# Expert rows beyond the first 128 in units of 32 rows, computed in float32 on four column tiles

## The reference, cut to what matters

```python
def expert_block(args):
    xb, e = args
    return (jax.nn.silu(xb @ w1_l[e]) * (xb @ w3_l[e])) @ w2_l[e]
```

```
135 135 153 129 194 186 171  89 103 161 174  73  77  88 155 115
145  78 135 127 141 177 113 138 161 102  85 101 134 120 112 105
```

## Time and profile before

| | |
|---|---|
| median of three runs | 2259.6 us |
| the profiled execution | 2255.27 us, of it 2253.7 us from the first to the last instruction (the span) |
| mean granted TensorE clock | 0.977 of 2.4 GHz |
| TensorE busy | 2149.3 us, 95% |
| VectorE, ScalarE, GpSimd busy | 1430.6, 971.0 and 581.7 us |
| moved by DMA | 407 MB, 181 GB/s over the span |

### The profile page before, as it was taken

One profiled execution on the slowest core, in us unless ns is written; L12 is line 12 of the kernel. 1 busy time (PEld: TensorE's weight loads), 2 busy tenths in 40 slices (PEclk: granted clock), 3 DMA queues, 4 the chain that ended last, 5 costly groups with the idle time before them and its releaser, 6 DMA issues. The chain is left out here.

```text
span 2253.7 us, 34056 instructions
## 1 busy us (share of the span) xinstructions
PE 2149.3 (95%) x10539; PEld 1773.2 (79%) x10540; DVE 1430.6 (63%) x2866; ACT 971.0 (43%) x1569; POOL 581.7 (26%) x595
## 2 busy tenths in 40 slices
PE   6999999999899999994889999999999999899998
PEld 5878888888788888884778888888888878767775
DVE  5788888888566665564536465665566566846554
ACT  4433344444432222222435465665556465623332
POOL 1121111111244333332121223233332132233332
PEclk9999999999999999996999999999999999999999
DMA  6111110132534333324787677898787778943441
GB/s 231 60 38 66 65 60 37 65 112 92 187 107 136 121 121 117 103 91 147 292 309 256 219 266 289 292 363 289 283 294 260 289 290 305 334 169 125 158 141 49
DMA packets 160333, 407.13 MB, mean 181 GB/s; under 512 B 18835, under 2 KB 22347, under 8 KB 160014
## 3 DMA queue, kind: packets, MB, share of 16 engines
q1 hardware_dynamic: 138518, 337.17, 42.0%
q0 software_dynamic: 14560, 43.11, 5.8%
q10 hardware_dynamic: 7200, 26.22, 2.9%
HBM read 330.12 MB, written 84.82 MB: 184 GB/s over the span
## 5 line engine op out<-in xcount | busy, mean ns | idle before, releaser
L234 PE MATMUL bank<-w_hi,mix_x 128*128 128x512 f32 x816 | 333.3, 408 | 9.9 <-DMA mix_x<-xT_dram 4.0
L236 PE MATMUL bank<-w_hi,mix_x 128*128 128x512 f32 x816 | 323.8, 397 | 0.0
L235 PE MATMUL bank<-w_lo,mix_x 128*128 128x512 f32 x816 | 322.9, 396 | 0.0
L2113 PE MATMUL bank<-w_hi,x_hi 128*128 128x512 f32 x784 | 307.6, 392 | 8.1 <-POOL w_lo L2070 4.6
L2212 DVE TENSOR_TENSOR w_lo<-raw,w_hi 128x2048 fp32r<-128x2048 f32 x130 | 292.6, 2311 | 34.8 <-ACT w_hi L2149 34.7
L2115 PE MATMUL bank<-w_hi,x_lo 128*128 128x512 f32 x784 | 307.1, 392 | 0.0
L2114 PE MATMUL bank<-w_lo,x_hi 128*128 128x512 f32 x784 | 307.1, 392 | 0.0
L2149 ACT ACTIVATE w_hi<-raw 128x2048 fp32r<-128x2048 f32 x130 | 238.8, 1925 | 4.8 <-DMA raw<-in_w 4.8
L2070 POOL TENSOR_TENSOR w_lo<-shared,w_hi 128x2048 fp32r<-128x2048 f32 x31 | 157.2, 5071 | 231.7 <-DMA shared<-hn_dram,entry 131.9
L234 PEld LDWEIGHTS bank<-w_hi,mix_x 128*128 128x128 f32 x816 | 156.7, 192 | 42.0 <-issue 5.1
L236 PEld LDWEIGHTS bank<-w_hi,mix_x 128*128 128x128 f32 x816 | 156.3, 192 | 34.7
(11 more groups left out here) (316 smaller groups left out, 4222.1 us busy)
## 6 DMA issues: line engine op xcount, KB each, us to landing
raw<-in_w SPq DMA_DIRECT2D x128, 1024.0 KB, 8.5
shared<-in_w SPq DMA_DIRECT2D x64, 1024.0 KB, 8.6
y_dram<-y_sb ACTq DMA_DIRECT2D x50, 512.0 KB, 6.9
xT_dram<-mix_x SPq DMA_DIRECT2D x34, 512.0 KB, 3.5
mix_x<-xT_dram SPq DMA_DIRECT2D x34, 512.0 KB, 4.5
shared<-in_w_in SPq DMA_DIRECT2D x24, 512.0 KB, 6.5
small<-in_x_prompt SPq DMA_DIRECT2D x16, 512.0 KB
xr_sb<-in_x_prompt SPq DMA_DIRECT2D x16, 512.0 KB
```

Of the source, the lines that this page charges most:

```text
L234: pe.matmul(bank[:, :], x_hi[:, k, :], wh[:, k, :], start=(k == 0), stop=False)
L235: pe.matmul(bank[:, :], x_hi[:, k, :], wl[:, k, :], start=False, stop=False)
L236: ins = pe.matmul(bank[:, :], x_lo[:, k, :], wh[:, k, :], start=False, stop=(k == KD - 1))
L2113: pe.matmul(bank[:, :], x_hi[:, k, :], wh[:, k, :], start=(k == 0), stop=False)
```

## The change

Every expert has one block of 128 rows now, and its rows beyond 128 go in units ("tails") of 32. `MAXT` is 32 + 4112/32 = 160. An expert has max(1, (rows - 128)/32 rounded up) units: also one with at most 128 rows has one, whose rows nothing reads. Units need no split weights: they multiply plain float32 rows with the raw matrices. All raw matrices stay whole for that: w1 and w3 of two experts (`raw13[0]` and `raw13[1]`), w2 of one (`raw2`). The units of expert e + 1 are computed within expert e's turn, between its H3 matmuls and its second half of Y; those of expert 0 in the turn of expert 31, for which its weights are loaded a second time. There are three slots of split weights in place of four. The first half of Y (12 matmuls, `first_down`) stands inside the unit's code, so it is done again by every unit after an expert's first.

```diff
-MAXBLK = NE + (SEQ + NS) * 2 // P
+TAIL = 32
+TILES = P // TAIL
+MAXT = NE + (SEQ + NS) * 2 // TAIL
-        y_dram = dram("y_dram", ((MAXBLK + 2) * P, D))
+        y_dram = dram("y_dram", (NE * P + (MAXT + 1) * TAIL, D))
...
# DVE, before the expert stage: units of each expert, at least one
-TS(blk[:, 0, :], POS, float(P - 1), None, ALU.add)
+TS(blk[:, 0, :], POS, float(TAIL - 1 - P), None, ALU.add)
-TS(blk[:, 1, :], blk[:, 0, :], 7, None, ALU.arith_shift_right)
+TS(blk[:, 1, :], blk[:, 0, :], 5, None, ALU.arith_shift_right)
 TS(rt[:, 0, :], blk[:, 1, :], 1.0, None, ALU.max)
...
# SP
+def expert(e, two, j):
+    wait_lo(sp_, e, 2, 1)
+    load(behind(e), 1 - j, 2)
+    sp_.wait_ge(h3_mm, e + 1)
+    for m in range(2):
+        if last(e):
+            load_gate(m)
+        else:
+            load(e + 2 if not isinstance(e, int) or e < NE - 2 else 0, j, m)
 sp_.wait_ge(rows_loaded, 16)
-for m in (1, 2):
-    for c in range(2):
-        load(0, m, c)
-reload(1)
-reload(2)
+load(0, 0, 1)
+sp_.wait_ge(lo_ready, 1)
+sp_.wait_ge(w1_lo, 1)
+load(0, 0, 2)
+load(1, 1, 0)
+load(1, 1, 1)
+for e in range(2):
+    expert(e, 0, e)
 total = count_all(sp_)
-with sp_.Fori(total + 1, MAXBLK + 2) as i:
-    sp_.dma_start(y_dram[bass.ds(i * P, P), :], hn_dram[0:P, :]).then_inc(spare_filled, 16)
+with sp_.Fori(total, MAXT + 1) as i:
+    sp_.dma_start(y_dram[bass.ds(i * TAIL + NE * P, TAIL), :], hn_dram[0:TAIL, :]).then_inc(spare_filled, 16)
 with sp_.Fori(0, total) as i:
     sp_.sem_inc(spare_filled, 16)
-with sp_.Fori(3, NE) as e:
-    reload(e)
+with sp_.Fori(1, NE // 2 - 1) as two:
+    for j in range(2):
+        expert(two * 2 + j, two, j)
...
# GpSimd, expert(e): one gather of the block's rows, then one for each unit, then its half of w1
+q = behind(e)
+first, end = span(pool, q)
+if not last(e):
+    gather(e + 1)
+with pool.Fori(first, end) as i:
+    ...
+    gather_tail(i + 1, at + (rest >> (12 * more)))
+if not last(e):
+    split_w1(e + 1, *follow(two, j))
...
# PE, a unit of expert e + 1 in expert e's turn
+def tail(i, e, two, j):
+    for m in range(2):
+        for c in range(2):
+            pe.wait_ge(*tail_in(e, two, j, m, c))
+    pe.wait_ge(t_x_in, i + 1)
+    w13 = raw13[1 - j][:, :].rearrange("p (m k n) -> p m k n", m=2, k=KD)
+    for k in range(KD):
+        for q in range(TILES):
+            ins = pe.matmul(UP_T[q * TAIL:(q + 1) * TAIL, :].rearrange("p (m n) -> p m n", m=2), xT_t[:, k, :],
+                            w13[:, :, k, q * P:(q + 1) * P], start=(k == 0), stop=(k == KD - 1))
+    ins.then_inc(t_up_mm, 1)
+    ...
+    pe.wait_ge(hidT_lo_ready, 2 * e + 2)
+    first_down(0)
+    pe.wait_ge(t_rows, 16 * i + 32)
+    first_down(1)
+    tail_transposes()
+    pe.wait_ge(t_hid, i + 1)
+    pe.transpose(HID_T, hid_t[:, :], ident[:, :]).then_inc(t_hid_tp, 1)
+    first_down(2)
+    first_down(3)
+    for c in range(2):
+        pe.wait_ge(*tail_in(e, two, j, 2, c))
+    pe.wait_ge(t_y_in, i + 1)
+    pe.wait_ge(t_hidT_in, i + 1)
+    ...
+    for k in range(KF):
+        for q in range(TILES):
+            ins = pe.matmul(DOWN_T[q * TAIL:(q + 1) * TAIL, :], hidT_t[:, k * TAIL:(k + 1) * TAIL],
+                            w2[:, k, q * width:(q + 1) * width], start=(k == 0), stop=(k == KF - 1))
+    ins.then_inc(t_down_mm, 1)
...
# ACT, expert(e)
+split(e, two, j, 2)
+act.wait_ge(h1_mm, e + 1)
+act.activation(tanh_h[:, :], H1[:, :], ACT.Tanh, scale=0.5)
+split(e + 1, *follow(two, j), 0)
+for n in range(2):
+    act.wait_ge(hid_tp, 2 * e + n + 1)
+    copy(hidT_hi[:, slice(*K_OF[n]), :], parts_of(AT[n], n))
+if not last(e):
+    x_halves(e + 1)
+with act.Fori(first, end) as i:
+    tail(i, e)                       # tanh, next rows, hidT_t, y_t and its store
+split(e + 1, *follow(two, j), 1)
+for n, done in enumerate((tails_done, y1_mm)):
+    act.wait_ge(done, e + 1)
+    copy(y_sb[:, n * 512:(n + 1) * 512], Y[n][:, :])
```

More of the change, by code:

```diff
@@ L1950, in span, with behind @@
+                (t_entry, t_rows, t_xtp, t_x_in, t_up_mm, t_tanh, t_up, t_hid, t_hid_tp, t_hidT_in, t_down_mm, t_y_in, t_stored) = [sem(n) for n in (
+                    "t_entry t_rows t_xtp t_x_in t_up_mm t_tanh t_up t_hid t_hid_tp t_hidT_in t_down_mm t_y_in t_stored").split()]
+                def behind(e):
+                    return 0 if isinstance(e, int) and e == NE - 1 else e + 1
                 def span(eng, e):
-                    first = eng.value_load(blk[0:1, 0, bass.ds(e, 1)], min_val=0, max_val=MAXBLK - 1)
@@ L2108, in block_of, with expert @@
+                        def expert(e, two, j):
+                            first, end = span(pe, behind(e))
+                            pe.wait_ge(xe_lo_ready, 2 * e + 2)
                             for m, (bank, done) in enumerate(((H1, h1_mm), (H3, h3_mm))):
@@ L2242, in choices_rows, with expert @@
                             dve.wait_ge(place_steps, 4)
-                            STT(yrow[:, :, :], rowbase[:, :, :], float(P), place[:, :, :], ALU.add, ALU.add).then_inc(place_steps, 1)
+                            STT(yrow[:, :, :], rowbase[:, :, :], float(-NE * (CAP - P) - P), place[:, :, :], ALU.add, ALU.add).then_inc(place_steps, 1)
                             dve.wait_ge(place_steps, 5)
-                        def after(e, j, end):
-                            if isinstance(e, int) and e == NE - 1:
+                        def expert(e, two, j):
+                            first, end = span(dve, behind(e))
+                            if last(e):
+                                dve.wait_ge(xe_tp, NE)
@@ L2248, in after @@
                                 choices_rows()
-                            for part in parts_ahead(e, j):
-                                theirs = part[2] == 0 and not (isinstance(e, int) and e + 2 == NE and part[0] == NE)
-                                split(*part, halves=(0,) if theirs else (0, 1))
-                        split(0, 0, 0)
+                            split(e, two, j, 2)
+                            dve.wait_ge(tanh_done, e + 1)
+                            STT(up[:, :], tanh_h[:, :], 1.0, H1[:, :], ALU.add, ALU.mult).then_inc(up_done, 1)
@@ L2254, in _ @@
+                            split(e + 1, *follow(two, j), 0, (0, 1) if last(e) else (0,))
+                            with dve.Fori(first, end) as i:
+                                tail(i)
+                            if not last(e):
+                                x_halves(e + 1)
+                            split(e + 1, *follow(two, j), 1)
+                        split(0, 0, 0, 0)
                         x_halves(0)
-                        split(0, 0, 1)
-                        split(0, 0, 2)
@@ L2257, in _ @@
-                        all_blocks(dve, block_of, after)
+                        split(0, 0, 0, 1)
+                        each_expert(dve, expert)
         with ExitStack() as late:
```

422 lines of the change are left out of this document (238 added, 184 removed).

## The result

| | kernel before | changed kernel | forecast |
|---|---|---|---|
| median of the runs, us | 2260.06 (2258.1 to 2264.37, 4 runs) | 2505.98 (2500.84 to 2513.0, 4 runs) | 2377 |
| ratio to before | 1 | 1.109 [1.105, 1.112] | 1.052 |
| span of the profiled execution, us | 2253.7 | 2511.3 | |
| expert stage, us | 904.0 | 1149.5 | 1021 |
| mean granted clock | 0.977 | 0.936 | |

What follows compares the result with a forecast made beforehand. TensorE was taken to bound the expert stage. Terms 7 + 100 - 7 + 2 + 4 + 11 = +117 us on 2255.3 make 2372; the median lies 4.3 higher, so 2377 us. Own range 2305 to 2430; 8-in-10 range 2295 to 2575.

Steps and rivals of the forecast that it cites:

- The other engines: Expert turns: ScalarE some 16 us, VectorE about the same, loads 20.8 us, all hidden under TensorE's 25.0 us; nothing charged.
- In order of time ScalarE is the closest: ScalarE's w3 high parts behind a unit's down: low part ready after about 7 us, H3 begins after 8.1; nothing charged.
- a wait for ScalarE in every turn, say: Example of outcomes lying between the forecast and rival 1, given a chance of 0.07.
- The start: First unit of the expert stage: TensorE waits for w3 of expert 1, +4 us.
- The fills: 121 fills on the SP queue delay w2 of expert 3, stalling TensorE in expert 2's turn, +100 us.
- Rival 3: The fills hold nothing up: 2275 us, or 2231 us with units at full streaming; chance 0.08.
- TensorE's work: Expert stage: 32 blocks, 40 units of 7.2 us and repeated `first_down`, 879 us in place of 872, +7 us.
- Rivals 1 and 2: Units' column tiles overlap by pairs only (2561 us, chance 0.27), or not at all (2940 us, chance 0.05).
- The issue rate: Units' matmuls: 0.071 us a record, so 64 up records take at least 4.5 us; 3.9 was taken.
- rival 1: Units' column tiles overlap by pairs only: up 7.0 us, unit 12.0 us, total 2561 us; chance 0.27.
- The end: Last turn: late gate load and split delay `first_down` by 9 us and the last `y_sb` by 2, +11 us.
- low end: Forecast's own range: 2305 us with full streaming, 82 us of fill stall and 5 at the end.

Runs made afterwards that it cites:

- run 2: Changed kernel with ScalarE splitting the next w2 right behind `y_sb`, ahead of its store and the register loads; 2471.8 us, ratio 1.094.
- run 5: Changed kernel with GpSimd's waits for gather landings moved to just ahead of the next list load; 2499.4 us, ratio 1.105.
- run 7: Changed kernel with both ScalarE's earlier w2 split and GpSimd's later landing waits; 2383.6 us, ratio 1.055.
- run 4: Changed kernel with 31 larger fills, earlier w2 split, first unit's transposes behind H3, last turn's gate splits behind its unit; 2397.0 us, ratio 1.060.
- run 8: Changed kernel with ScalarE's and GpSimd's orders mended, fills in the mixer's 16 steps, last turn and start reordered; 2278.4 us, ratio 1.008.
- run 12: Changed kernel with ScalarE's and GpSimd's orders, last turn and start mended, and one 512 KB fill behind each turn's loads; 2261.5 us, ratio 1.0002.
- run 1: Changed kernel with 31 fills of 512 KB in place of 121 of 128 KB; 2432.8 us, ratio 1.076.
- run 6: Changed kernel with all fills moved to the token mixer's stage, 322 rows in each of 16 steps; 2413.6 us, ratio 1.068.
- run 3: Changed kernel with column tiles outermost in the up matmuls, k inside; 2790.9 us, ratio 1.235.
- run 9: As run 8, with the mixer's fills in its first 14 steps, 368 rows each; 2283.6 us, ratio 1.010.

## Why the prediction was right and wrong

**The failed step: "The other engines", and in it "In order of time ScalarE is the closest … I charge nothing; if it came 1 us late in each turn it would cost 32."** The turn was taken as TensorE's 25.0 us. ScalarE's order of time was worked out for one place, the low part of w3 at H3, and from busy time alone ("six halves, 11.6, plus 2.8 plus some 1.5 for the unit on ScalarE, 16 us"). That busy time was right, 15.6 us. What it left out is what the profile does not count as busy: the unit's store (1.07 us of issue, 1.56 with the loop), `y_sb`'s store and three register loads (3.21). And it stopped at H3, where the low part was all but in time; the next link, w2's split, then `tanh_h`, w2's low part and `hid`, came 2.2 to 3.0 us late in 30 turns. One-unit turns are 4.5 us longer than the forecast's, the regular turns 122 us in all, where the price named was 32; the clock that fell behind some of these waits (0.94 in the second window of the changed kernel) is in it. Runs 2, 5 and 7 show the cause and its size: with both queues put in order the same turns are 25.5 us, 3.9 less. The 0.5 that is left is no ring: TensorE is busy for 25.1 us of such a turn and waits some 0.4 for a low part. The prediction did name "a wait for ScalarE in every turn, say", within a chance of 0.07.

**A second ring that the forecast had no term for.** GpSimd's list loads, gathers and their landings are 28 us from split to split (run 2's timeline). It stayed hidden in the changed kernel (run 5 gained 7 us) and capped run 2 at 34 of 90 us. My expectations for runs 2 and 4 repeated the forecast's mistake one engine further on. It also makes the first turn longer: run 5 takes 12.5 us out of it.

**The start: +4 forecast, 12.5 ahead of the first H1 and some 10 in the first turn.** The term priced w3's bytes. TensorE in fact waited for the first unit's rows, whose list GpSimd asks for only when the block's rows have landed:

```profile
1072.25 1.06 PE L2171 MATMUL bank<-ident,rows_t 32*128 32x32 f32 x8 [12.38 <-DMA rows_t<-hn_dram,entry_t]
```

Putting these transposes behind H3 (runs 4, 8 and 12) lets H1 begin 7 to 12 us earlier and lengthens the first turn by 8 to 10, so none of the runs gains this term back.

**The fills: right in mechanism and size.** 106.7 us against +100, an iteration of 0.985 us against 0.975, and a gap that ends 7.9 us after w2's load is issued. Rival 3 is out. That they cost nothing when spread (run 12) fits the DMA share of 0.80; run 1 is left with a gap of 32 us at a share of 0.95 to 0.99, and the mixer of run 6 is 16 us longer.

**TensorE's work: right.** Up 3.66 us (3.9), down 1.93 (1.9), the small transposes and `hid`'s about 1.0 (1.0), one-unit turn without waits 25.5 (25.0), with two units 34.4 (34.9). Rivals 1 and 2 are out: 7.0 and 13.7 us were their up. The issue rate of 0.071 us a record that the sum took from rows 4 as a floor ("at least 4.5 us") did not hold for these records: 64 in 3.66 us are 0.057 each. The 3.9 lay under that floor by choice, not by a row.

The Trainium skill, page "TensorE: Matmul & The Clock Gate", section "The mechanism", has matmuls start and end strictly in program order; by that rule the prediction had rival 1 as the case. It wasn't: from 1589.543 on, four records start within 20 ns and the next four 0.24 us later, though each matmul is two records. (I take each group as one record of each tile, since a single tile's are 0.216 us apart in run 3.) Whole matmuls can still be in order there, a few ns apart. In run 3 they aren't: a new tile's records begin at 1880.84, and the tile before it starts its last three at 1881.05, 1881.27 and 1881.48. The same page's speedup of 2.38 with three tiles (section "Measured speedup vs the span model") is 0.79 of the ideal; four tiles gave 13.7 / 3.66 = 3.7 here, 0.94 of it.

**The end: right.** 9.1 us ahead of the last `first_down` against +9, and the late stage's first transposes wait 8.0 us, 6.0 before, against +2. A further 3.7 us before the hid transposes wasn't forecast. VectorE works out where each row's results lie (2185.22 to 2189.61) ahead of w2's low part in that turn, and run 12 has the same 3.7 us.

**The forecast's own range.** Its low end adds up to 2309 us, not 2305: 2377 less 44, 18 and 6. Nothing hangs on it.

What stays open: whether the slower list writes are what makes the mixer wait for `idx` when it carries the fills (runs 6, 8 and 9, 16 to 22 us at a DMA share of 0.3 to 0.4), and what each of the ring's two gaps on ScalarE is worth alone. VectorE's place in the ring was not tried either: `tanh_h` is done at 1585.30, but `up` starts at 1587.46, behind w2's low part. Leaving the fills out was not tried.

## What to carry to other kernels

Write down the ring of every engine that is touched, not its busy time: from one turn's event through everything on its queue, with the DMA issues, register loads, loop ends and waits for landings that the profile calls "issue" or idle, back to the same event. Where two rings have nearly one length, mending either alone gives little (7 and 34 us here, 122 for both), so list them all before you price an edit. A DMA that nobody waits for is best given to the queue one at a time behind the transfers that are needed: filling these rows (16 to 21 MB) cost 107, 32, 16 to 22, and 0 us in four ways. And look at both sides of a wait that an edit takes away: at the start of this stage it only moved.

## What the runs showed of the hardware

- Four column tiles of 32 stationary columns stream together in plain float32: 64 records of 256 columns in 3.66 us, and 12.25 us with each tile's records in one piece.
- TensorE's granted clock can fall behind a wait of only 2 to 3 us. Not every one did it: the turn from 1573.9 has one of 2.5 us and kept 1.00, the next has one of 3.0 us and 0.94, run 2's second window one of 2.0 us and 0.89. In run 7, without these waits, the clock is 1.00 from 1300 to 2050.
- VectorE's and GpSimd's subtractions of a half matrix don't run beside each other: the one that starts first runs through, and the other waits for it. In the changed kernel all 23 of VectorE's that start within one of GpSimd's end 2.15 us after it (alone they take 2.29), and GpSimd's keep their 4.6. In the kernel before, where VectorE's starts first by 0.35 us, GpSimd's takes 6.4 us. VectorE's on `raw` took 2.89 us in the mean in the changed kernel, 2.31 before. One pair:

```profile
1589.08 4.57 POOL L2126 TENSOR_TENSOR w_lo<-raw,w_hi 128x2048 fp32r<-128x2048 f32 x1 [7.79 <-ACT w_hi L2259]
1590.65 5.15 DVE L2343 TENSOR_TENSOR w_lo<-raw,w_hi 128x2048 fp32r<-128x2048 f32 x1
```

- A store of 128 KB that scatters four column tiles to rows takes ScalarE's queue 1.07 us to issue, one of 512 KB in whole rows 0.36.
